# Adding squared tiles in pairs on GpSimd ahead of the sum over partitions, in four projection jobs

## The reference, cut to what matters

```
def rmsnorm(x, g):
    xf = x.astype(F32)
    y = xf * lax.rsqrt(jnp.mean(xf * xf, axis=-1, keepdims=True) + RMS_EPS)
    return (y * g.astype(F32)).astype(x.dtype)

h = h + rmsnorm(y @ w_out, g_post)          # S5 layer (post0), FoX layer (post1)
x = x + gate * (merged @ w_out)             # hybrid layers; then rms_norm(x, g)
                                            # of layer 1 (pre_l1), or g_final (final)
```

## Time and profile before

| what | value |
|---|---|
| median of three runs | 3727.47 us (3722.4, 3727.47, 3731.34) |
| profiled execution, span | 3729.7 us |
| TensorE busy | 3197.5 us (86%) |
| VectorE busy | 2483.3 us (67%) |
| ScalarE busy | 1446.9 us (39%) |
| GpSimd busy | 133.6 us (4%) |
| mean granted TensorE clock | 0.916 |
| L1279, sums of squares | 128 instructions, 39.7 us of matmul, mean 392 ns |

### The profile page before, as it was taken

One profiled execution on the slowest core, in us unless ns is written; L12 is line 12 of the kernel. 1 busy time (PEld: TensorE's weight loads), 2 busy tenths in 40 slices (PEclk: granted clock), 3 DMA queues, 4 the chain that ended last, 5 costly groups with the idle time before them and its releaser, 6 DMA issues. The chain is left out here.

```text
span 3729.7 us, 56483 instructions
## 1 busy us (share of the span) xinstructions
PE 3197.5 (86%) x22836; PEld 2750.2 (74%) x22836; DVE 2483.3 (67%) x3383; ACT 1446.9 (39%) x1764; POOL 133.6 (4%) x218
## 2 busy tenths in 40 slices
PE   7982210997999997999999999998999999999998
PEld 6872210886878876888888777887888888777887
DVE  6449999767776756576777656775565575655564
ACT  4330100443344543333444444344333454444343
POOL 0000000000000000000000000000000000000000
PEclk9975555998999998999999999999999999999999
DMA  5520000765766443566667435764544454434453
GB/s 196 184 78 2 2 1 23 250 240 176 265 236 242 175 148 146 199 248 240 216 237 259 147 125 201 261 253 175 185 177 158 158 215 181 147 125 180 170 192 113
DMA packets 101036, 645.70 MB, mean 173 GB/s; under 512 B 11360, under 2 KB 12000, under 8 KB 36704
## 3 DMA queue, kind: packets, MB, share of 16 engines
q1 hardware_dynamic: 70880, 513.23, 38.2%
q0 software_dynamic: 27648, 100.68, 7.5%
q10 hardware_dynamic: 2304, 28.84, 1.9%
HBM read 628.02 MB, written 14.68 MB: 172 GB/s over the span
## 5 line engine op out<-in xcount | busy, mean ns | idle before, releaser
L1256 PE MATMUL acc<-xs,whi 128*128 128x512 f32 x7216 | 2602.2, 404 | 102.1 <-DVE xs L818 90.2
L1258 PE MATMUL acc<-xs,wlo 128*128 128x256 f32 x7216 | 2037.5, 282 | 0.0
L1256 PEld LDWEIGHTS acc<-xs,whi 128*128 128x128 f32 x7216 | 1371.7, 190 | 444.7 <-issue 96.0
L754 DVE TENSOR_TENSOR wlo<-raw,whi 128x2048 fp32r<-128x2048 f32 x459 | 1051.8, 2292 | 534.2 <-ACT whi L410 534.2
L1258 PEld LDWEIGHTS acc<-xs,wlo 128*128 128x128 f32 x7216 | 1380.5, 191 | 6.0 <-issue 3.6
L410 ACT ACTIVATE whi<-raw 128x2048 fp32r<-128x2048 f32 x459 | 875.0, 1907 | 0.0
L431 ACT ACTIVATE acctmp<-acc 128x256 f32<-128x256 f32 x563 | 215.0, 383 | 1454.8 <-PE acc L1258 1437.8
L793 DVE TENSOR_TENSOR w<-acc,acctmp 128x256 f32<-128x256 f32 (+1 forms) x496 | 209.4, 423 | 526.5 <-ACT acctmp L431 525.3
L785 DVE SCALAR_TENSOR_TENSOR modacc<-modw,cact,modacc 128x1024 f32<-128x1024 f32 x192 | 245.4, 1278 | 12.7 <-DMA modw<-in_modstream 11.2
L389 POOL DMA_DIRECT2D modw<-in_modstream x192 | 101.6, 529 | 1778.7 <-DVE modacc L785 1041.7
L1370 PE MATMUL acc<-state,ct 128*32 128x64 f32 x512 | 10.8, 262 | 152.2 <-DVE state L870 152.2
(11 more groups left out here) (227 smaller groups left out, 2261.5 us busy)
## 6 DMA issues: line engine op xcount, KB each, us to landing
raw<-in_wstream SPq DMA_DIRECT2D x483, 1024.0 KB, 4.8
modw<-in_modstream POOLq DMA_DIRECT2D x192, 512.0 KB, 4.7
residual<-h ACTq DMA_DIRECT2D x2, 2048.0 KB, 6.3
ga_gate<-w ACTq DMA_DIRECT2D x2, 2048.0 KB, 10.6
gated_retention<-w ACTq DMA_DIRECT2D x2, 2048.0 KB, 8.2
w<-gated_retention ACTq DMA_DIRECT2D x2, 2048.0 KB, 9.3
h<-residual ACTq DMA_DIRECT2D x2, 2048.0 KB, 12.5
w<-ga_gate ACTq DMA_DIRECT2D x2, 2048.0 KB, 10.6
```

Source lines behind the costliest of these rows:

```text
L754: dve.tensor_tensor(out=wlo[s % SPL][:, :], in0=raw[s % RAW][:, :], in1=whi[s % SPL][:, :].bitcast(F32), op=ALU.subtract).then_inc(w_lo_do ...
L1256: pe.matmul(acc[par % 2][0:cols, :], whi[w][:, c:c + cols], x_split[:, k, :, :], start=(k == 0), stop=False, skip_group_check=True)
L1258: mm = pe.matmul(acc[par % 2][0:cols, 0:T], wlo[w][:, c:c + cols], x_split[:, k, 0, :], start=False, stop=(k == kts - 1), skip_group_check ...
```

## The change

GpSimd gets a function `pair_squares(name, j)` for odd j: it waits for the square of tile j and adds tile j onto tile j - 1 in place. It is called eight times for each of the four norms. For `post0` the calls are woven into the DMA issues of `s5out`, whose loop is written out; for `post1` they stand ahead of the issues of the job `rv`; for `pre_l1` and `final` after the last issue. TensorE's `sum_tile` is called for odd tiles alone, waits for the pair, and counts two tiles as used; its calls sit in side(2), side(4) to side(14), and after the job. ScalarE's wait for a free slot is rounded to pairs.

```
--- before.py
+++ after.py
@@ -105,6 +105,7 @@
     return out
 
 
+PAIRED = ["post0", "post1", "pre_l1", "final"]
 NORM_NO = {n: i for i, (n, _, _) in enumerate(NORMS)}
 SQ_BEFORE = running([(n, k) for n, k, _ in NORMS])
 SPLIT_BEFORE = running(SPLITS)
@@ -388,7 +389,24 @@
                 src = modstream[m] if isinstance(m, int) else modstream[bass.ds(m, 1), :, :].rearrange("a p n -> (a p) n")
                 pool.dma_start(modw[s][:, :], src).then_inc(mod_loaded[s], 16)
 
+            def pair_squares(name, j):
+
+                pool.wait_ge(sq_done, SQ_BEFORE[name] + j + 1)
+                pool.tensor_tensor(out=stg_tiles[:, j % 8 - 1, :], in0=stg_tiles[:, j % 8 - 1, :], in1=stg_tiles[:, j % 8, :],
+                                   op=ALU.add).then_inc(sem("sq_paired"), 1)
+
             for c in range(len(MOD_JOBS)):
+                if MOD_JOBS[c] == (None, "s5out"):
+                    for j in range(MOD_STEPS):
+                        pool.wait_ge(mod_acc, j + (MOD_STEPS + 1) * c)
+                        load(MOD_STEPS * c + j, j % 2)
+                        if j % 2 and j > 1:
+                            pair_squares("post0", j - 2)
+                    pair_squares("post0", KT - 1)
+                    continue
+                if MOD_JOBS[c] == (0, "rv"):
+                    for j in range(1, KT, 2):
+                        pair_squares("post1", j)
                 if c == 0:
                     load(0, 0)
                     load(1, 1)
@@ -397,6 +415,10 @@
 
                         pool.wait_ge(mod_acc, i * 2 + (s + (MOD_STEPS + 1) * c))
                         load(i * 2 + (s + MOD_STEPS * c), s)
+            for j in range(1, KT, 2):
+                pair_squares("pre_l1", j)
+            for j in range(1, KT, 2):
+                pair_squares("final", j)
 
 
         @block.scalar
@@ -439,7 +461,7 @@
                 def side(j):
                     act.wait_ge(ready, n0 + j + 1)
                     if j >= 8:
-                        act.wait_ge(sq_used, SQ_BEFORE[name] + j - 7)
+                        act.wait_ge(sq_used, SQ_BEFORE[name] + j // 2 * 2 - 6)
                     act.activation(stg_tiles[:, j % 8, :], buf[:, j, :], ACT.Square).then_inc(sq_done, 1)
                 return side
 
@@ -1275,12 +1297,12 @@
 
             def sum_tile(name, j):
 
-                pe.wait_ge(sq_done, SQ_BEFORE[name] + j + 1)
-                pe.matmul(bank[0][:, 0:T], part[:, :], stg_tiles[:, j % 8, :], start=(j == 0), stop=(j == KT - 1),
-                          skip_group_check=True).then_inc(sq_used, 1)
+                pe.wait_ge(sem("sq_paired"), KT // 2 * PAIRED.index(name) + j // 2 + 1)
+                pe.matmul(bank[0][:, 0:T], part[:, :], stg_tiles[:, j % 8 - 1, :], start=(j == 1), stop=(j == KT - 1),
+                          skip_group_check=True).then_inc(sq_used, 2)
 
             def sum_side(name):
-                return lambda j: sum_tile(name, j - 1) if j else None
+                return lambda j: sum_tile(name, j - 1) if j and j % 2 == 0 else None
 
             def rms(name, staging):
```

## The result

The changed kernel took 3736.81 us (median of 7 runs, 3732.4 to 3741.45) against 3726.56 (7 runs, 3721.74 to 3731.34). The ratio is 1.0031, 95% interval 1.0022 to 1.0041: slower by 11.6 us, 8.2 to 15.3. The forecast was +6.2, 3733.7 us. The profiled execution's span is 3732.6 us and its device time 3734.72.

The account below looks back on a forecast made before the run. TensorE's matmuls were taken to bound the kernel. Inside the jobs -3.0, -3.0 and +6.4, at the ends +1.8, +2.0, +0.8 and +1.3, unrounded +6.2 us, gave 3733.7 us; range 3726 to 3742 us.

Parts of the forecast that it names:

- The mechanism: In four jobs, fewer sums free TensorE if GpSimd's pair is ready before demand; otherwise TensorE waits; +6.2 us in all.
- the sign: Whole kernel: leaning to slower, +6.2 us or +0.17%; slower 41%, faster 8%.
- no measurable change: Whole kernel: the change stays below about 0.2% (7.5 us), what a measurement can tell; chance 51%.
- Inside `s5out` and `foxout`: Between tiles of these jobs: 7 sums fewer, the held pair still in time, so each job gains 3.0 us.
- The cover: In `s5out`: the pair is ready at 775.34 and TensorE asks at 775.58, leaving 0.24 us and no stall.
- Inside the `out` jobs: Between tiles: TensorE stands 0.82 us for each of 7 pairs, +3.2 us per job, +6.4 for both.
- the time from the square to the sum: Handing on to GpSimd 0.08, add 0.68, handing back 0.05: 0.81 us, if GpSimd starts at once.
- The ends: Last pair before L809: `s5out` +1.8, `foxout` +2.0, first `out` +0.8, second `out` +1.3 us.
- First rival: In `s5out` and `foxout`, VectorE does not hold GpSimd: +2.6 us in all, 3730.1 us; chance 10%.
- Second rival: In `s5out`, VectorE's queued L785 runs ahead of the add: +13.6 us in all, 3741.1 us; chance 9%.
- Third rival: The pair is ready in time in all four jobs, only the ends cost: -9.9 us, 3717.6 us; chance 7%.
- The beat: Jobs run at 5.55 or 5.64 us per tile; 5.64 between sums gives +8.7, 3736.2 us; counted within the forecast's 74%.

Follow-up runs that it names:

- the copy: Changed kernel with GpSimd copying tile j over tile j - 1 in place of adding; ran once, 3741.0 us.
- the memset: Changed kernel with GpSimd writing ones over the slot of tile j - 1 in place of adding; ran once, 3726.11 us.
- the late sums: Changed kernel with TensorE taking each pair's sum one tile later in the two `out` jobs; 3716.99 us, ratio 0.9979 to before.

## Why the prediction came out as it did

The mechanism was right at each step that the traces show, and the sign. The size was short, and the change is a measurable slowdown where no measurable change was the likeliest case. That case also rested on 7.5 us as the least that can be told from nothing; with 7 runs of each kernel the interval reaches 3.5 us to either side, so even the +6.2 of the forecast would have shown.

- Inside `s5out` and `foxout`: -3.0 forecast, -3.16 measured. The pair is held by the weight split and still comes in time. A held add ended 0.60 us behind the weight split where 0.54 was taken. The cover was thinner than the 0.24 us of the forecast: with what the hand-over really takes it is 774.31 - 774.08 - 0.14 = 0.09 us.
- Inside the `out` jobs: +3.2 forecast, +4.2 and +4.3 measured. TensorE asked when the square ended, as worked out (2508.02 against 2508.03 there). The mis-sized term is the time from the square to the sum, 0.81 us in the forecast. It is 0.94: the add started 0.08 behind the square, as taken; it took 0.72 in place of 0.68; and from its end to TensorE's start are 2508.98 - 2508.84 = 0.14 us where I took 0.05 from ScalarE's hand-over to TensorE. That is 0.13 us more, and the forecast said that this term counts 18 times: 2.3 us, which takes +6.2 to +8.5 against +8.4 measured in the jobs and ends. That the two meet so closely is in part luck: the `out` jobs took 2.1 us more than forecast where 14 of these terms make 1.8, the ends 0.3 where 4 make 0.5, and `s5out` and `foxout` gained 0.2 more.
- The ends: +1.8, +2.0, +0.8, +1.3 forecast, +1.92, +2.05, +0.86, +1.37 measured. At the kernel's end the pause before the last sum grew from 1.47 to 2.79 us and not to the 2.3 of the forecast, since the sum behind tile 15 is gone from there too; the time to L831 doesn't change by that. The slow sum there is not a sure thing: behind the same pause of 2.79 us it took 1.19 us in the profile of the changed kernel (end 4.05) and 0.67 in its repeat (end 3.53, where the repeat was expected to hold 4.05 to 0.3 us).
- First rival (GpSimd not held): false, shown by the add, the copy and the memset. Second rival (VectorE keeps its turn): false; L807 let the waiting add through. Third rival (the pair in time everywhere): false for this kernel; the late sums made it true inside the jobs (85.8 and 86.1 us in the `out` jobs).
- The beat: in `k` and `retproj` it changes between two executions of one program. Tiles with no sum between tiles with one ran at 5.55 in the first two jobs, and at 5.54 to 5.66 in the `out` jobs.
- What remains, some 3 us of the 11.6, is in no step of the forecast; the interval reaches down to 8.2.

## What to carry to other kernels

Before moving work off the bounding engine, compare two times in the trace: when the engine will ask for the result once the work is gone (it asks earlier, by what was taken away), and when the result's last input is ready. In the `out` jobs the two were 0.01 us apart, so the helper's whole latency became idle time of the bounding engine, and moving the use by one tile, or the input by one instruction, turned a loss of 0.3% into a gain of 0.1 to 0.2%. The last element of a reduction is best left off the detour, since nothing covers it.

## What the runs showed of the hardware

- VectorE's `tensor_tensor` with two inputs in SBUF holds a GpSimd instruction that reads SBUF until it ends, 2.5 us for an add of 0.72 and 2.2 for a copy of 0.40; a GpSimd memset beside it took 0.31 us. The waiting GpSimd instruction then goes ahead of VectorE's next one, which took 1.76 us in place of 1.28.
- From the end of a GpSimd add to TensorE's start took 0.14 us; from the end of ScalarE's square, in the kernel before, 0.06.
- One program has two beats, 5.55 and 5.65 us per tile of 32 matmuls, which differ between executions and change from job to job, and in the changed kernel's `out` jobs also from tile to tile; two profiles of one kernel lay 8.6 us apart.
- Behind the same 1.86 us of idle TensorE, the first tile of one job ran at a granted clock of 0.77 in one execution of a program and of 1.00 in another, and took 7.45 and 5.83 us.
